# Output projection of a gated conv/pool decoder layer: residual and turned tile moved from the engines to DMAs

## What is computed

```python
def rmsnorm(x, g):
    xf = x.astype(jnp.float32)
    r = lax.rsqrt(jnp.mean(xf * xf, axis=-1, keepdims=True) + EPS)
    return (xf * r * g.astype(jnp.float32)).astype(x.dtype)

    merged = gates[..., :D_MODEL] * ya + gates[..., D_MODEL:] * yb
    x = x + rmsnorm(merged @ w_o, g_post_mix)

    h2 = rmsnorm(x, g_pre_mlp)
    f = jnp.square(jax.nn.relu(h2 @ w_up)) @ w_down
    x = x + rmsnorm(f, g_post_mlp)
```

## Time and profile before

| | us |
|---|---|
| median of 3 runs (997.85 to 999.02) | 998.44 |
| profiled execution | 997.95 |
| its span on the slowest core | 996.9 |
| spans of all eight cores | 996.4 to 996.9 |
| TensorE busy | 979.6 |
| VectorE, ScalarE, POOL busy | 473.5, 323.2, 230.1 |

### The profile page before, as it was taken

The page is one execution under the profiler, slowest core; times in us unless marked ns, Lnnn a source line. Parts: engine busy times, 40 slices in busy tenths (PEclk is TensorE's granted clock), DMA queues, the critical chain, the costliest instruction groups (busy, mean ns, idle before and its releaser), DMA issues.

```text
span 996.9 us, 16428 instructions; the slowest of 8 cores (996.4 to 996.9 us)
## 1 busy us (share of the span) xinstructions
PE 979.6 (98%) x5463; PEld 484.9 (49%) x5463; DVE 473.5 (47%) x858; ACT 323.2 (32%) x639; POOL 230.1 (23%) x362
## 2 busy tenths in 40 slices
PE   7999999999999999999999999999999999999997
PEld 6544444444444444444445545555445555544444
DVE  4667855334634331251667886533365444301413
ACT  4422232227633333201333224222584333301111
POOL 7111211115421132032113242111362111120110
PEclk9999999999999999999999999999999999999999
DMA  9999999991782239489856366964209422231342
GB/s 216 177 179 143 123 135 129 115 155 29 117 130 82 74 95 234 148 211 146 201 80 78 54 83 86 258 91 65 37 8 127 89 66 73 74 117 43 94 118 85
DMA packets 46690, 113.76 MB, mean 114 GB/s; under 512 B 7056, under 2 KB 9360, under 8 KB 46352
## 3 DMA queue, kind: packets, MB, share of 16 engines
q0 software_dynamic: 40272, 91.51, 55.5%
q1 hardware_dynamic: 6048, 20.91, 6.7%
q10 hardware_dynamic: 288, 0.30, 0.1%
HBM read 164.20 MB, written 18.49 MB: 183 GB/s over the span
## 4 chain that ended last, share of the span: by engine, by line
PE 94%; issue 1%; DMA 1%; DVE 1%; ACT 1%; POOL 1%; DVEq 0%; ACTq 0%; POOLq 0%
PE PS L135 93%; DMA WS<-w_in 1%; ACT TM L152 1%; PE PS L139 1%; DVE AR L155 1%; POOL AR L155 0%; DVE TM L165 0%; ACT AR L152 0%; POOL AR L126 0%; ACT STAT L152 0%; DVE AR L165 0%; DVE STAT L442 0%; POOL WS L126 0%; DVEq L220 0%; DVE TM L155 0%
## 5 line engine op out<-in xcount | busy, mean ns | idle before, releaser
L135 PE MATMUL PS<-AR,WS 128*128 128x512 bf16 (+1 forms) x3664 | 656.6, 340 | 2.9 <-DVE STAT L442 1.6
L135 PEld LDWEIGHTS PS<-AR,WS 128*128 128x128 bf16 x3664 | 321.1, 98 | 328.8 <-issue 4.8
L135 PE MATMUL PS<-WS,AR 128*128 128x512 bf16 (+1 forms) x1392 | 296.2, 374 | 0.0
L152 ACT ACTIVATE TM<-PS 128x512 f32<-128x512 f32 (+3 forms) x252 | 140.3, 570 | 351.3 <-PE PS L135 349.4
L135 PEld LDWEIGHTS PS<-WS,AR 128*128 128x128 bf16 x1392 | 135.8, 98 | 154.3
L155 DVE TENSOR_TENSOR AR<-TM 128x512 bf16<-128x512 f32 (+1 forms) x200 | 120.1, 615 | 137.7 <-ACT TM L152 133.2
L126 POOL DMA_DIRECT2D WS<-wd_bf x96 | 51.8, 540 | 267.9 <-PE PS L135 261.3
L152 ACT ACTIVATE TM<-PS,CS 128x512 f32<-128x512 f32 (+1 forms) x80 | 49.6, 623 | 131.5 <-PE PS L135 123.5
L126 POOL DMA_DIRECT2D WS<-w_in x96 | 52.6, 556 | 165.3 <-PE PS L135 164.7
L442 DVE RECIPROCAL STAT<-STAT 128x1 f32<-128x1 f32 (+1 forms) x54 | 8.7, 162 | 135.2 <-ACT STAT L152 135.0
L155 DVE TENSOR_TENSOR TM<-PS,TM 128x512 f32<-128x512 f32 (+1 forms) x40 | 24.4, 610 | 95.3 <-PE PS L135 94.4
(11 more groups left out here) (62 smaller groups left out, 337.2 us busy)
## 6 DMA issues: line engine op xcount, KB each, us to landing
WS<-w_in POOLq DMA_DIRECT2D x96, 256.0 KB, 8.9
WS<-wd_bf POOLq DMA_DIRECT2D x96, 256.0 KB, 3.2
WS<-w_up POOLq DMA_DIRECT2D x64, 256.0 KB, 7.3
wd_bf<-w_dn POOLq DMA_DIRECT2D x8, 1024.0 KB, 37.2
y_p<-AR SPq DMA_DIRECT2D x15, 512.0 KB, 5.0
AR<-x_p SPq DMA_DIRECT2D x9, 512.0 KB, 15.2
WS<-w_oc POOLq DMA_DIRECT2D x16, 256.0 KB, 16.0
WS<-w_o POOLq DMA_DIRECT2D x16, 256.0 KB, 26.2
```

The source lines that it names most:

```text
L135: return self.add("pe", lambda e: e.matmul(out, lhsT, rhs, start=start, stop=stop), reads=[lhsT, rhs], writes=[out], signal=sig, name="mm")
L152: return self.add("act", lambda e: e.activation(out, in_, func, **kw), reads=rd, writes=wr, name=name)
```

## The change

Stage 3 alone is touched. The residual addition on POOL becomes a DMA from `XT` that accumulates into `x1`, issued on POOL's queue. `g_pre_mlp` is loaded once a pass as a row broadcast to all partitions (`GPM`), on SP's queue. The statistics of `x1` and the scaling are a function `s3_h`, two tiles behind the matmuls: square and root on ScalarE, reciprocal on VectorE, then one scalar_tensor_tensor on VectorE that multiplies by the reciprocal and by `GPM`. A DMA with transpose on SP's queue turns the bf16 tile into `hT`. The transposes on TensorE and the copy out of PSUM go. The roots are no longer shared by two statistics. `XT` has three buffers instead of two, and the three buffers of `XN` and `GPM` lie in the region of `ApT`, which is free by then.

```diff
--- before.py
+++ after.py
@@ -330,6 +330,7 @@
     scT = din("scT", [128, KC, 32])
     spT = din("spT", [128, KC, 240])
     cst = din("cst", [128, 64])
+    g_pre_mlp = din("g_pre_mlp", [D])
     g_post_mix = din("g_post_mix", [D])
     g_post_mlp = din("g_post_mlp", [D])
     w_in = din("w_in", [48, 128, 1024])
@@ -398,8 +399,9 @@
         USX = [_view(AR, S0 + 9728 + i * 1472, F32, [16, 23]) for i in range(2)]
         PSX = _view(AR, S0 + 12672, F32, [16, 23])
         QSX = _view(AR, S0 + 14144, F32, [16, 23])
-        XT = [tmv(i * 4096, F32, [D]) for i in range(2)]
-        XN = [tmv(8192 + i * 2048, BF16, [D]) for i in range(2)] + [_view(AR, A_AP + 8 * TMAX, BF16, [D])]
+        XT = [tmv(i * 4096, F32, [D]) for i in range(3)]
+        XN = [_view(AR, A_AP + i * 2048, BF16, [D]) for i in range(3)]
+        GPM = _view(AR, A_AP + 6144, F32, [D])
         XN0 = [_view(AR, A_MG + i * 2048, BF16, [D]) for i in range(2)]
         JUNK = tmv(12288, BF16, [D])
         RL = [tmv(14336 + i * 2048, F32, [512]) for i in range(3)]
@@ -820,15 +822,7 @@
 
 
 
-            nxt = {}
-
-            def s3_cols(i):
-                if i not in nxt:
-                    if stat_ctr[0] % 2:
-                        stat_ctr[0] += 1
-                    nxt[i] = stat()[0]
-                    stat()
-                return nxt[i]
+            P.dma("sp", GPM, bass.AP(g_pre_mlp.tensor, 0, [[0, 128], [1, D]]), "gpm", name="gpm")
 
             def s3_mm(i):
                 b = banks.pair()
@@ -836,63 +830,35 @@
                     for ki, k in enumerate(JORDER):
                         P.mm(PS[:, b + nh, :], mgT[:, k, i * 128:(i + 1) * 128],
                              W.rhs((ps_i, "o", nh * 4 + k // 2))[:, k % 2, :], start=(ki == 0), stop=(ki == KC - 1))
-                    if nh == 0 and i >= 4:
-                        s3_T(i - 4)
-                return b
-
-            def s3_sq(h):
-                c = s3_cols(h + 2) + 1
-                P.act(JUNK, x1[:, h, :], AF.Square, scale=1.0 / 32.0, accum_out=STT_[:, c:c + 1], name="sq")
-
-            def s3_xn(h):
-                c = s3_cols(h + 2) + 1
-                P.act(XN[h % 3], x1[:, h, :], AF.Identity, scale=STT_[:, c:c + 1], name="xn")
-
-            def s3_root(h):
-                c = s3_cols(h + 2) + 1
-                rstd(STT_[:, c:c + 1])
-
-            def s3_step(i):
-                b = s3_mm(i)
-                c = s3_cols(i)
                 pm = bass.AP(PS, b * 512, [[4096, 128], [1, D]])
-                P.act(JUNK, pm, AF.Square, scale=1.0 / 32.0, accum_out=STT_[:, c:c + 1], name="sq")
-                rstd(STT_[:, c:c + (2 if i >= 2 else 1)])
-                xt = XT[i % 2]
-                P.stt("dve", xt, pm, STT_[:, c:c + 1], GBC[:, 0, :], ALU.mult, ALU.mult, name="mixn")
+                _, ss = mean_sq(JUNK, pm)
+                rstd(ss)
+                xt = XT[i % 3]
+                P.stt("dve", xt, pm, ss, GBC[:, 0, :], ALU.mult, ALU.mult, name="mixn")
                 banks.give(b, b + 1)
-                P.tt("pool", x1[:, i, :], x1[:, i, :], xt, ALU.add, name="x1")
-                if i >= 1:
-                    s3_sq(i - 1)
-                if i >= 2:
-                    s3_xn(i - 2)
-
-            def s3_T(i):
-                transposes(XN[i % 3], hT, i * 128, C_GPL)
+                P.dma("pool", x1[:, i, :], xt, "acc%d" % i, name="x1", accum_op=ALU.add)
+
+            def s3_h(i):
+                _, ss = mean_sq(JUNK, x1[:, i, :])
+                rstd(ss)
+                P.stt("dve", XN[i % 3], x1[:, i, :], ss, GPM, ALU.mult, ALU.mult, name="xn")
+                P.dma("sp", hT[:, :, i * 128:(i + 1) * 128], XN[i % 3], "tr%d" % i, name="h2T", transpose=True)
 
             def s4_first(f):
                 s4_unit(f, tgs[0])
 
             P.act(cs(65), cs(64), AF.Sqrt, name="warm")
             for i in range(NT):
-                s3_step(i)
+                s3_mm(i)
+                if i >= 2:
+                    s3_h(i - 2)
             for k in range(8):
                 W.free((ps_i, "o", k))
-            s3_T(NT - 4)
-            s3_root(NT - 2)
-            s3_xn(NT - 2)
+            s3_h(NT - 2)
             s4_first(0)
             s4_first(1)
-            s3_T(NT - 3)
-            s4_first(2)
-            s3_sq(NT - 1)
-            s3_root(NT - 1)
-            s3_xn(NT - 1)
-            s3_T(NT - 2)
-            s4_first(3)
-            s4_first(4)
-            s3_T(NT - 1)
-            for f in range(5, 8):
+            s3_h(NT - 1)
+            for f in range(2, 8):
                 s4_first(f)
             for f in range(32):
                 for seg in tgs:
@@ -1074,6 +1040,7 @@
                           f(inputs["pool_scale"]).reshape(8, 128)], axis=0).T
     shared = {
         "cst": f(cst),
+        "g_pre_mlp": f(inputs["g_pre_mlp"]).reshape(D),
         "g_post_mix": f(inputs["g_post_mix"]).reshape(D),
         "g_post_mlp": f(inputs["g_post_mlp"]).reshape(D),
         "w_in": cols(inputs["w_in"][0]),
```

## The result

The changed kernel took 1028.16 us (1026.59 to 1029.16, 4 runs) beside 998.73 us before, a ratio of 1.0295 with a 95% interval of 1.0277 to 1.0312.

The account below looks back on a forecast made before the run. TensorE, busy 98% of the span, was taken as the bound. Added waits less gains, 4.4 + 7.0 - 5.4 = +6.0 us and 9.6 - 6.0 = +3.6 us, put +9.6 on 998.44: 1008.0 us, 8 in 10 between 989 and 1110.

Parts of the forecast that it names:

- four named places: TensorE's waits for turned tiles in the up projection: 4.4 and 7.0 us in pass 0, 0.95 and 3.5 plus 5.2 in pass 1.
- the sum: The likeliest case, chance 0.36: added waits less time gained, +6.0 us in pass 0 and +3.6 in pass 1, 1008.0 us.
- the clock: TensorE's granted clock in idle stretches of 5 us and more; not shown by the rows, so given no size.
- What is taken away, 11.4 us: Transposes and their waits leave TensorE in the output projection: 5.4 us in pass 0 and 6.0 in pass 1, at most.
- VectorE and ScalarE fit in 3.45 us a tile: In the output projection ScalarE needs about 3.0 us a tile and VectorE 2.9, within TensorE's 3.45.
- E(i+1) = E(i) + 3.45: In the output projection the first square of each tile on ScalarE starts 3.45 us after that of the tile before.
- L: Time from POOL's issue of the accumulating DMA to its landing, taken as 5.5 us; below 4.9 would bring nothing more.
- T: Time to landing of the DMA that turns a tile into hT, taken as 5.7 us: 3.5 of transfer plus 2.2.
- The first waits: TensorE waits for tile 3 at the start of the up projection: 4.4 us in pass 0, 0.95 in pass 1.
- The last tiles, doubled by the loads: Eight w_up loads make each pass's last two turning DMAs occupy queues 7 us, not 3.5; waits 7.0, then 3.5 and 5.2.
- Rival A: Accumulating and turning DMAs are quick (under 4.9 and 2.2 us), few waits: -8.1 us, 990.3 us; chance 0.30.
- Rival D: Turning DMAs go one after the other, at 9.3 or 12.1 us a tile, and set the end: 1089 or 1137 us; chance 0.24.

Follow-up runs that it names:

- filling experiment: Changed kernel plus dummy identity matmuls on TensorE ahead of the four places where it waits for turned tiles: 1028.71 and 1030.83 us, ratio 1.0314.

## Why the prediction was right or wrong

The sign was right, the size was not: +9.6 us were forecast and +29.4 us measured, within the wide range. The mechanism, waits for turned tiles at four named places, was the right one. Two steps failed: the sum lets every tile's squares start on time, 3.45 us apart, and it prices the accumulation at 5.5 us throughout. The runs showed ScalarE standing behind late accumulations, so that tiles started up to 5.7 us late, and accumulations of 9.0 us at the start and 9.8 us beside the loads. A third term, the clock, was left out.

- *What is taken away, 11.4 us.* Held: without the residual, when nothing else was late, 10.3 us were gained with 1.7 us of wait left.
- *VectorE and ScalarE fit in 3.45 us a tile.* By their work they do: in the changed kernel `xn` took 1.28 us as assumed, and without the residual nothing in the projection was late. VectorE's part held only because POOL's addition had gone, which the prediction didn't see.
- *The start of a tile, E(i+1) = E(i) + 3.45.* This failed. The prediction names ScalarE's wait for the accumulation, with the next tile's square behind it, and puts it at nothing. It was 4.49 us for tile 0 (core 4); its own limit says why, since an L above 4.9 us uses up ScalarE's slack and L was 8.95.
- *L, 5.5 us.* 4.7 us without turning DMAs, 7.6 us in the changed kernel. The first one took 8.95 us on this core and 5.0 to 7.1 us on the others, with no turning DMA yet on the queues. The prediction took the queues for empty by the earlier trace rows, but that row begins at 235 us and the first accumulation is issued at 228.5. For the time before, the trace of the kernel before has:

```profile
221.60:235.00 13.40, 13.40 (x63) 6.08 (x62) 5.57 (x9) 6.17 (x14) 5.23 (x3) 1.00 0.55 81
```

  A share of 0.55 from loads of `w_up`. The changed kernel adds the load of `GPM`, costed at nothing, which took from 220.8 to 231.2 us. Which of the two delays the first accumulation no run separates.
- *T, 5.7 us.* 3.0 to 3.2 us alone, so too dear by nearly a factor of two: 1056 packets, close to the 1024 assumed, but 0.020 us each instead of 0.055. Beside accumulations it took 5.1 to 7.1 us in pass 0 and 4.9 to 7.7 in pass 1, so the 5.7 us come out near the truth by two errors that cancel, the price of a packet and the company of the other DMA. Both DMAs were priced as if they never met. In the changed kernel, issued at 246 to 249 us and then at 262 to 270 us (KB, us to landing; packets, MB, share of the queues; q0 has the loads and the accumulation of tile 7):

```profile
AR<-TM POOLq DMA_DIRECT2D x2, 512.0 KB, 7.7
AR<-AR SPq DMA_TRANSPOSE x1, 7.1
...
q0 software_dynamic: 508, 1.17, 99.8%
q1 hardware_dynamic: 207, 0.05, 7.6%
...
WS<-w_up POOLq DMA_DIRECT2D x4, 256.0 KB, 17.5
```

- *The first waits.* Measured from E(3) at TensorE's pace, tile 3 of pass 0 was in `hT` 5 us later than the + 18.2 of the sum: 3.9 us for the late square on ScalarE, 1.2 us for T (6.9 us), 0.4 us on the way to the accumulation, less 0.6 us for its L (4.9 us). In pass 1 its square was on time, L was 6.7 and T 6.3 us, 2.3 us later in all. The waits were 9.6 and 3.5 us where 4.4 and 0.95 stand in the sum.
- *The last tiles, doubled by the loads.* From E(7) of pass 0 the last tile took 35.1 us where 25.2 stand in the sum. The square was 5.7 us late, the steps to the accumulation took 0.7 us more, and the accumulation, beside the loads, 9.8 us instead of 5.5. The part that was priced as doubled, from the scaled tile to its landing, took 12.0 us, 4.5 us held on SP and 7.5 us to landing, against 12.7 in the sum. In pass 1 the last tile took 31.4 us, of which that part is 12.8. This agreement is luck. The factor of two was taken from a transfer of 4 KB rows (4.6 to 9.3 us, rows 9), while the turning DMAs of the tiles just before landed in 15.4 to 20.9 us, five to seven times the 3.0 to 3.2 us of one that is alone, and the quiet T that was doubled was too long. The waits were 8.8 and 12.4 us, where 7.0 and 8.7 stand in the sum. Holding the loads back gave 25.6 us, a little more than these two waits (21.2 us); the first waits were 1.5 us shorter in sum, and what is left may be the clock behind the waits, which was not measured by itself.
- *Left out: the clock.* The balance leaves 7.9 us to it. By the filling experiment most of that is no separate loss.
- *Excess in one line:* waits 34.3 instead of 21.1 us (+13.2, of them 7.8 in the two first waits and the rest in the two second ones) and 7.9 us of clock, together 21.1 us, against the 21.2 us between the span's growth of 30.8 and the forecast 9.6.
- *Rival A* had the true T and failed by the company that the DMA keeps. The estimate that stands there from the Trainium skill, "DMA: Bandwidth & Descriptors", section "Latency and other measured facts", is 3.0 us; the traces agree with it, 3.0 to 3.2 us alone. *Rival D* asked for more than 3.45 us that doesn't overlap; the turning DMAs of the projection overlapped and followed their tiles, 2.9 to 5.6 us apart, without bringing the projection to a stand, and it fell, as did the figure of 10.5 us a tile.

## What to carry to other kernels

A DMA of small packets that is put in the path of the last tiles must not meet bulk loads: order the loads behind it, or leave these tiles on the engine. Price a DMA that is issued once a tile together with the other DMAs of the same tile and with what is still on the queues when the first one starts, not against the empty queue of the kernel before. Where an engine that runs in order waits for such a DMA, count what is queued behind the wait: here a late sum of the first tile made the later tiles late too. And before an operation moves from PSUM to SBUF operands on VectorE, look what POOL reads at that time.

## What the runs showed of the hardware

- A transposing DMA of 128 x 1024 bf16 from SBUF to SBUF is 1056 packets, 1.2 us of issue on SP and 3.0 to 3.2 us to landing when alone; beside accumulating DMAs 4.9 to 7.7 us; issued beside eight loads 15.4 to 20.9 us, with SP's issue held for up to 11.5 us, and the one issued last of all 7.2 to 7.5 us (profiled core).
- An accumulating DMA of 512 KB within SBUF lands in 4.7 us without turning DMAs (median), in 6.7 to 8.4 us beside them in pass 1, and in 9.8 us beside eight loads; its issue takes POOL 0.86 us, against 0.53 us for a load.
- VectorE's scalar_tensor_tensor with two SBUF tensors took 3.3 to 3.4 us beside POOL's addition of 2.35 us and 1.28 us without it; tensor_scalar 2.8 and 0.75 us. POOL's own time didn't change.
- TensorE's granted clock fell to between 0.65 and 0.77 in waits of 9 to 12 us and was at 0.70 to 0.82 in the 10 to 17 us after, and at 0.90 in the 15 us after a wait of 3.5 us; full is 2.4 GHz, and the mean of a stretch mixes it with the lower level of 1.2 GHz.
